# First projection pieces loaded among the gate pieces, a gate sent later, and a branch product on other accumulators

## The chip, the cores and the metric

The kernel runs on one core of a Trainium2 chip, as one program launched once. The metric is the device time in microseconds from the program's first to its last instruction with what the launch adds around them. A profiled execution gives a trace of every instruction and transfer. The engines are PE (TensorE), DVE (VectorE), ACT (ScalarE), POOL (GpSimd) and SP (SyncE, which here only issues loads).

## What is computed

A trunk of two layers over 256 tokens of width 1024, all in float32. Each layer has a token mixer and then a channel mixer, and each of the two is framed by a modulation that comes from a conditioning vector `c`:

```
shift, scale, gate = split(silu(c) @ w_mod + b_mod)
h   = normalize(x) * (1 + scale) + shift
x   = layer_norm(alpha * x + (1 + gate) * f(h))
```

The token mixer projects `h` by one matrix `w_in` (1920 columns), runs three branches on the result (stick-breaking attention, trailing pooling, sliding-window attention), projects each branch to 1024 columns, and merges them with gates:

```
qa, ka, va, u, qc, kc, vc = split(h @ w_in)
g_a, g_b, g_c = split(sigmoid(h @ w_gate))
merged = g_a * (y_a @ w_branch_a) + g_b * (y_b @ w_branch_b) + g_c * (y_c @ w_branch_c)
f(h) = merged @ w_out
```

The channel mixer is a dense SwiGLU in layer 0 and a top-2-of-8 expert SwiGLU in layer 1.

## The kernel before

All weights come from memory in pieces of 1 MB (128 partitions x 2048 floats) through a ring of `RING = 6` slots in `w_raw`. SP issues them in one fixed order. It waits, before each, until the slot's old piece is used: `piece_used` is counted up by DVE, `split_used` by PE, `shift_used` by PE for the shift pieces of the first modulation. As SP runs its queue in order, a load that waits holds back every load behind it.

A piece for an accurate product is split in two: ACT rounds it to `w_hi` (L577), DVE takes the rest to `w_lo` (L973, counts up `piece_used`), and PE makes three matmuls for each product: hi by hi, lo by hi and hi by lo (L1573 to L1575). The first `UNSPLIT = 3` pieces of a stretch are not split; PE multiplies them as they are (`project_raw`, L1584), each of these matmuls being two records in the trace. Tokens are in two tiles of 128 rows, t = 0 and 1.

The first modulation (`MOD0`) has twelve pieces. Its order is shift, scale, shift, scale, ... (eight pieces) and then the four gate pieces. The shift pieces are multiplied by PE (L1636), scale and gate pieces by DVE, four steps each into `mod_acc` (L1001, `mod_piece`). Then:

- PE sends shift and scale to all partitions (L1641, L1644); DVE's `modulate` makes `h` for tile 0 and tile 1 (L1054, L1057); PE transposes a tile (`h_transposed`, L1596); ACT keeps it as `actT_raw` (L606) and rounds it (L615).
- `send_gate` (L1609) sums the gate over the partitions into two banks of the accumulator memory, and ACT's `keep_gate` copies them to `gate1` (L599).
- After that GpSimd fills `mod_acc` anew for the next modulation: it waits for `gate1_ready`, issues four small loads, clears `mod_acc` (L478 to L480) and loads the next bias into it (L486, `acc_ready`). The pieces of that next modulation stand among the projection pieces, one after in3, one after the piece behind it, and so on. DVE's first step on the first of them waits for `acc_ready`, and DVE takes the pieces strictly in order.

The accumulator memory `ps` has eight banks of 512 columns. The projection of column block n and tile t goes to bank `2t + n % 2`. In the gate phase that leaves banks 0 and 2 (even blocks) and banks 1 and 3 (odd blocks) to be read by ACT's sigmoid (L746), which counts up `gate_ready` once for each tile: 12 in a layer, the last two for block 5, an odd one.

After the gates come the branch products. Their pieces carry the numbers j = 19 to 22. Piece 19 makes the products of branches 0 and 1 for the first 512 columns, piece 20 those for the other 512, pieces 21 and 22 those of branch 2. DVE multiplies the gates by the sums of each (`gated_branch`, L1190; `branch_read` counts the reads), merges them (L1255), and PE transposes the merged rows (L1756). A DVE helper `after(j)` is run three pieces behind the piece that DVE splits.

## Time and profile before

| what | value |
|---|---|
| median of three runs | 1730.75 us (1728.66 to 1731.32) |
| the profiled execution's own time | 1730.3 us |
| its span, first to last instruction | 1728.5 us |
| TensorE, busy | 1634.3 us, 95% of the span |
| VectorE, busy | 1360.6 us, 79% |
| ScalarE, busy | 1021.0 us, 59% |
| GpSimd, busy | 109.6 us, 6% |
| TensorE's mean granted clock | 0.985 |
| moved from memory | 510.46 MB, 301 GB/s over the span with what is written |

The times in the rows below are microseconds from the span's start. A timeline row is a run of like instructions: start, length, engine, line, operation, output and inputs, count, and in brackets the idle time ahead of it with what ended it. PEclk is the granted clock as a share of 2.4 GHz: 0.50 is 1.2 GHz, and a number between is a second in which both levels occurred. Instructions overlap a little in the records, since the end of a matmul is modelled.

### The profile page before, as it was taken

Reading aid. Unit: us, or ns where it says so; the run is one execution under the profiler, and the core shown is the slowest. Engines: PE = TensorE matmul, PEld = TensorE weight load, DVE = VectorE, ACT = ScalarE, POOL = GpSimd, SP = SyncE. Lnnn points to the kernel's source line nnn. Section 1 sums busy time; section 2 is a strip of 40 time slices with the busy share of each in tenths; the row PEclk is TensorE's granted clock in tenths of the full one; section 3 lists DMA queues with packets and bytes.
Section 4 is the critical chain, followed back from the end, with each engine's and each line's share of the span. In section 5 each row is a group of like instructions: output and inputs, shape, how many; then the busy total and the mean of one; then the engine's idle time right before and its main releaser. Section 6 shows DMA issues by size and latency. Waiting matters only on the chain.

```text
span 1728.5 us, 20762 instructions
## 1 busy us (share of the span) xinstructions
PE 1634.3 (95%) x7272; PEld 1274.2 (74%) x7273; DVE 1360.6 (79%) x1158; ACT 1021.0 (59%) x824; POOL 109.6 (6%) x76
## 2 busy tenths in 40 slices
PE   5999899999999999999999989999899999999895
PEld 2587767888587766777888768888687777788673
DVE  5696877665796877899888986565689999988798
ACT  1375434343375434778777775445577878877573
POOL 1200010000100002002001010000200200200200
PEclk9999999999999999999999999999999999999998
DMA  9775747775576644999999986666699999999993
GB/s 363 270 249 194 267 147 260 278 289 195 177 273 209 224 165 158 384 398 375 375 370 376 395 334 237 218 220 218 230 379 398 387 393 395 382 369 358 390 393 121
DMA packets 215859, 510.41 MB, mean 295 GB/s; under 512 B 12473, under 2 KB 16745, under 8 KB 215810
## 3 DMA queue, kind: packets, MB, share of 16 engines
q1 hardware_dynamic: 208770, 496.15, 79.0%
q0 software_dynamic: 7040, 13.60, 2.3%
q8 instruction: 31, 0.51, 0.1%
q14 instruction: 18, 0.14, 0.0%
HBM read 510.46 MB, written 10.49 MB: 301 GB/s over the span
## 4 chain that ended last, share of the span: by engine, by line
PE 76%; DVE 9%; DMA 7%; ACT 4%; issue 3%; SPq 0%; DVEq 0%; ACTq 0%
PE ps L1573 18%; PE ps L1575 17%; PE ps L1574 17%; PE ps L1579 5%; PE ps L1580 5%; DMA w_raw<-in_exp_w_dram 4%; PE ps L1584 4%; DVE w_lo L1426 3%; ACT w_hi L841 3%; PE ps L2110 2%; PE ps L2081 1%; DMA w_raw<-in_w_mod_mix_dram 1%; DVE w_lo L973 1%; PE ps L1615 1%; DMA w_raw<-in_w_gate_dram 1%
## 5 line engine op out<-in xcount | busy, mean ns | idle before, releaser
L1426 DVE TENSOR_TENSOR w_lo<-w_raw,w_hi 128x2048 fp32r<-128x2048 f32 x332 | 756.5, 2289 | 121.7 <-ACT w_hi L841 120.9
L841 ACT CAST w_hi<-w_raw 128x2048 fp32r<-128x2048 f32 x332 | 632.2, 1912 | 177.0 <-DMA w_raw<-in_exp_w_dram 161.8
L1573 PE MATMUL ps<-w_hi,actT_hi 128*128 128x512 f32 (+1 forms) x1464 | 581.0, 397 | 37.1 <-DVE w_lo L1426 15.9
L1575 PE MATMUL ps<-w_hi,actT_lo 128*128 128x512 f32 (+1 forms) x1464 | 567.6, 388 | 0.0
L1574 PE MATMUL ps<-w_lo,actT_hi 128*128 128x512 f32 (+1 forms) x1464 | 567.4, 388 | 0.0
L1573 PEld LDWEIGHTS ps<-w_hi,actT_hi 128*128 128x128 f32 x1464 | 277.2, 189 | 109.7 <-DVE w_lo L1426 30.1
L1575 PEld LDWEIGHTS ps<-w_hi,actT_lo 128*128 128x128 f32 x1464 | 277.1, 189 | 57.2
L1574 PEld LDWEIGHTS ps<-w_lo,actT_hi 128*128 128x128 f32 x1464 | 277.5, 190 | 53.8 <-issue 1.7
L973 DVE TENSOR_TENSOR w_lo<-w_raw,w_hi 128x2048 fp32r<-128x2048 f32 x82 | 187.5, 2288 | 91.2 <-ACT w_hi L577 91.0
L577 ACT CAST w_hi<-w_raw 128x2048 fp32r<-128x2048 f32 x82 | 156.0, 1907 | 110.3 <-DMA w_raw<-in_ffn_w_dram 59.4
L1579 PE MATMUL ps<-w_hi,gT_hi 128*128 128x512 f32 x448 | 178.4, 398 | 3.5 <-DVE gT_hi L1453 1.9
L1580 PE MATMUL ps<-w_lo,gT_hi 128*128 128x512 f32 x448 | 177.1, 395 | 0.0
L1001 DVE SCALAR_TENSOR_TENSOR mod_acc<-w_raw,c_act,mod_acc 128x512 f32<-128x512 f32 x176 | 120.0, 745 | 10.7 <-DMA w_raw<-in_w_mod_mix_dram 7.1
L1579 PEld LDWEIGHTS ps<-w_hi,gT_hi 128*128 128x128 f32 x448 | 84.1, 188 | 29.4 <-DVE w_lo L1426 5.6
L1580 PEld LDWEIGHTS ps<-w_lo,gT_hi 128*128 128x128 f32 x448 | 84.2, 188 | 19.1
L537 POOL DMA_INDIRECT by_row<-hbuf,row_of x14 | 32.1, 2293 | 817.6 <-DVE hbuf L1512 606.2
L1584 PE MATMUL ps<-w_raw,actT_raw 128*128 128x512 f32 x144 | 65.4, 609 | 4.8 <-DMA w_raw<-in_w_in_dram 4.0
L1584 PEld LDWEIGHTS ps<-w_raw,actT_raw 128*128 128x128 f32 x144 | 27.5, 194 | 38.9 <-issue 36.8
L1573 PE MATMUL ps<-w_hi,gT_hi 128*128 128x512 f32 x136 | 54.2, 398 | 1.2 <-DVE gT_hi L1453 1.2
L1574 PE MATMUL ps<-w_lo,gT_hi 128*128 128x512 f32 x136 | 54.1, 398 | 0.0
L1575 PE MATMUL ps<-w_hi,gT_lo 128*128 128x512 f32 x136 | 53.5, 394 | 0.0
L1579 PE MATMUL ps<-w_hi,actT_hi 128*128 128x512 f32 x112 | 44.4, 397 | 3.4 <-DVE actT_hi L1469 3.4
(288 smaller groups left out, 1230.7 us busy)
## 6 DMA issues: line engine op xcount, KB each, us to landing
w_raw<-in_exp_w_dram SPq DMA_DIRECT2D x336, 1024.0 KB, 7.6
w_raw<-in_ffn_w_dram SPq DMA_DIRECT2D x33, 1024.0 KB, 5.1
w_raw<-in_w_mod_mix_dram SPq DMA_DIRECT2D x24, 1024.0 KB, 7.5
w_raw<-in_w_mod_ffn_dram SPq DMA_DIRECT2D x24, 1024.0 KB, 6.6
w_raw<-in_w_gate_dram SPq DMA_DIRECT2D x24, 1024.0 KB, 5.1
w_raw<-in_w_in_dram SPq DMA_DIRECT2D x14, 1024.0 KB, 5.3
w_raw<-in_w_out_dram SPq DMA_DIRECT2D x8, 1024.0 KB, 5.1
w_raw<-in_w_branch_c_dram SPq DMA_DIRECT2D x4, 1024.0 KB, 7.4
```

The lines of the kernel that those rows point to most:

```text
L577: nc.scalar.copy(w_hi[:, (j - stretch.raw) % SPLIT, :], w_raw[:, slot, :]).then_inc(split_hi, 1)
L841: nc.scalar.copy(w_hi[:, i % SPLIT, :], w_raw[:, slot, :]).then_inc(split_hi, 1)
L973: TTn(w_lo[:, slot, :], w_raw[:, slot, :], w_hi[:, (j - stretch.raw) % SPLIT, :].bitcast(F32), ALU.subtract).then_inc(piece_used, 1)
L1001: ins = STT(acc, w[:, k, n * BANK:(n + 1) * BANK], c_act[:, 2 * (q % 4) + k:2 * (q % 4) + k + 1], acc, ALU.mult, ALU.add)
L1426: TTn(w_lo[:, slot, :], w_raw[:, slot, :], w_hi[:, i % SPLIT, :].bitcast(F32), ALU.subtract).then_inc(piece_used, 1)
L1573: MM(to, hi, w_h, start=first, stop=False)
L1574: MM(to, hi, w_l, start=False, stop=False)
L1575: return MM(to, lo, w_h, start=False, stop=last)
L1579: MM(to, packed, w_h, start=first, stop=False)
L1580: return MM(to, packed, w_l, start=False, stop=last)
L1584: return MM(to, actT_raw[:, k, t * P:(t + 1) * P], w_raw[:, slot, at * width:(at + 1) * width], start=first, stop=last)
L2110: MM(bank(n), gT_lo[:, 0, 2 * h + part, :], split_piece(EXPERT, i, part, n * BANK, D)[0], start=False, stop=False)
```

## The change

In the start, SP loads the three unsplit projection pieces in0, in1 and in2 among the gate pieces of the first modulation: in0 and in1 behind the first gate piece, in2 behind the second. DVE modulates tile 1 after the first gate piece instead of before it. PE transposes tile 1 and multiplies it by in0 before it sends the gate, which now goes to banks 6 and 7 instead of 2 and 3, and ACT keeps it after tile 1's rows. The attention scores of layer 0, which use those banks, wait for `gate1_ready`.

In both layers, the first branch's product goes to banks 0 and 2 and the second's to banks 1 and 3 (before: 0 and 1, 2 and 3). The first waits for ten of the twelve sigmoids, the second for all. The product of piece 20 that goes to banks 0 and 1 waits until two gated products have been read instead of one.

```diff
@@ -162,6 +162,7 @@
 
 MOD0 = Stretch(mod_stream())
 MOD0.n_used = MODS - MOD_SHIFT
+IN_AMONG_GATES = {2 * MOD_SHIFT: (0, 1), 2 * MOD_SHIFT + 1: (2,)}
 MIX = Stretch(mix_stream(), raw=UNSPLIT)
 DENSE_PANELS, _dense = ffn_stream(D_FF, True)
 DENSE = Stretch(_dense, raw=UNSPLIT, first_slot=MIX.n % RING)
@@ -195,6 +196,7 @@
 HALF_P = P // 2
 FOLDS = 2 * len(EXPERT_PANELS)
 LOGITS = 4
+BRANCH_BANKS = {"even": (0, 2), "odd": (1, 3), 0: (0, 1), 2: (2, 3), 4: (4, 5)}
 NOWHERE = 1 << 20
 TURN_FREE, TURN_LATE = (2, 3), (5, 7)
 
@@ -426,9 +428,11 @@
                 for d, s in pairs:
                     sp.dma_start(d, s).then_inc(raw_loaded[slot], 16)
 
-            def stream(stretch, base, layer, before, split_base, expert=None, mod_layer=None):
+            def stream(stretch, base, layer, before, split_base, expert=None, mod_layer=None, begun=0):
 
                 for i, piece in enumerate(stretch.pieces):
+                    if i < begun:
+                        continue
                     old = before.pieces[before.n - RING + i] if i < RING else stretch.pieces[i - RING]
                     if old[0] == "mod":
                         sp.wait_ge(piece_used, base + i + 1 - (0 if i < RING else stretch.raw))
@@ -454,9 +458,14 @@
                     else:
                         sp.wait_ge(shift_used, before // 2 + 1)
                 load(i % RING, piece, ("mix", 0))
-            sp.wait_ge(shift_used, MOD_SHIFT)
+                if i == 2 * MOD_SHIFT:
+                    sp.wait_ge(shift_used, MOD_SHIFT)
+                for m in IN_AMONG_GATES.get(i, ()):
+                    sp.wait_ge(piece_used, MOD0.n_used + m + 1)
+                    load(MIX.slot(m), MIX.pieces[m], 0)
             for layer in range(DEPTH):
-                stream(MIX, layer * LAYER_PIECES + MOD0.n_used, layer, DENSE if layer else MOD0, layer * LAYER_SPLITS, mod_layer=("ffn", layer))
+                stream(MIX, layer * LAYER_PIECES + MOD0.n_used, layer, DENSE if layer else MOD0, layer * LAYER_SPLITS, mod_layer=("ffn", layer),
+                       begun=0 if layer else UNSPLIT)
                 if layer < 1:
                     stream(DENSE, MOD0.n_used + MIX.n_used, 0, MIX, MIX.n_split, mod_layer=("mix", 1))
                 else:
@@ -654,8 +663,8 @@
             for t in range(TT):
                 root(t + 1, t)
             turned_h(0, 0, 0)
-            keep_gate(0, 0)
             turned_h(0, 1, 0)
+            keep_gate(0, 4)
 
             for layer in range(DEPTH):
                 sbase = layer * LAYER_SPLITS
@@ -1130,8 +1139,9 @@
                     mod_piece(MOD0, i, [0] * RING, 0, 0, 0)
                 if i == 2 * MOD_SHIFT - 1:
                     dve.wait_ge(mod_sent, 1)
-                    for t in range(TT):
-                        modulate(chain, t, 4)
+                    modulate(chain, 0, 4)
+                if i == 2 * MOD_SHIFT:
+                    modulate(chain, 1, 4)
             rest_of_turned(0, 0, raw_met, 1)
 
             for layer in range(DEPTH):
@@ -1183,11 +1193,11 @@
                     step(nc.vector.reciprocal(rden, den))
                     TTn(scores[:, :, :], scores[:, :, :], rden.unsqueeze(2).broadcast_to([P, 8, P]), ALU.mult).then_inc(prob_ready, 1)
 
-                def gated_branch(n, br, first_bank):
+                def gated_branch(n, br, banks):
 
                     for t in range(TT):
                         gate = gates[:, t, br * D + n * BANK:br * D + (n + 1) * BANK]
-                        ins = TTn(gate, gate, bank(first_bank + t), ALU.mult)
+                        ins = TTn(gate, gate, bank(BRANCH_BANKS[banks][t]), ALU.mult)
                     ins.then_inc(branch_read, 1)
                     dve.wait_ge(branch_read, layer * 6 + BRANCH_ORDER.index((br, n)) + 1)
 
@@ -1228,8 +1238,8 @@
                         dve.wait_ge(gate_ready, layer * 12 + 12)
                         yT_rest(1)
                         dve.wait_ge(split_used, sbase + 20 + SPLIT)
-                        gated_branch(0, 0, 0)
-                        gated_branch(0, 1, 2)
+                        gated_branch(0, 0, "even")
+                        gated_branch(0, 1, "odd")
                         for t in range(TT):
                             ins = TTn(gate_columns(0, 0, t), gate_columns(0, 0, t), gate_columns(0, 1, t), ALU.add)
                         step(ins)
@@ -1764,6 +1774,8 @@
                                 ins = TR(ps[:, 4 + c // 2, (c % 2) * SEQ + t * P:(c % 2) * SEQ + (t + 1) * P], proj[:, t, c * P:(c + 1) * P], ident)
                         ins.then_inc(aT_sent, 1)
                     if j == 5:
+                        if layer < 1:
+                            pe.wait_ge(gate1_ready, 1)
                         stick_scores()
                     if j == 9:
                         suffix_sums()
@@ -1810,11 +1822,14 @@
                         send_gate(2, 0)
                 ins.then_inc(raw_met, 1)
                 if layer < 1:
-                    pe.wait_ge(piece_used, MOD0.n_used + RING)
-                    send_gate(0, 0)
-                second_tile(layer * 2, 0)
+                    h_transposed(0, 1, 2)
+                else:
+                    second_tile(2, 0)
                 for i in range(UNSPLIT):
                     project_raw(i, 1).then_inc(split_used, 1)
+                    if layer < 1 and i == 0:
+                        pe.wait_ge(piece_used, MOD0.n_used + RING)
+                        send_gate(0, 4)
 
                 for i, piece in enumerate(MIX.pieces):
                     if piece[0] == "mod" or i < UNSPLIT:
@@ -1844,21 +1859,23 @@
                         if j == 19:
                             pe.wait_ge(yT_hi_ready, layer * 2 + 1)
                             pe.wait_ge(yT_lo_ready, layer * 2 + 1)
-                            pe.wait_ge(gate_ready, layer * 12 + 12)
+                            pe.wait_ge(gate_ready, layer * 12 + 10)
                         if j == 20:
                             pe.wait_ge(pT_ready, layer * 2 + 2)
                         if j == 21:
                             pe.wait_ge(yT_hi_ready, layer * 2 + 2)
                             pe.wait_ge(yT_lo_ready, layer * 2 + 2)
 
-                        groups = {19: [(0, (0, 1), 0, 0), (1, (2, 3), 2, 0)], 20: [(0, (0, 1), 4, 0), (1, (2, 3), 0, 1)],
+                        groups = {19: [(0, (0, 1), "even", 0), (1, (2, 3), "odd", 0)], 20: [(0, (0, 1), 4, 0), (1, (2, 3), 0, 2)],
                                   21: [(2, (4, 5, 6, 7), 2, 2)], 22: [(2, (4, 5, 6, 7), 0, 3)]}[j]
-                        for br, ks, first_bank, read in groups:
+                        for br, ks, banks, read in groups:
                             if read:
                                 pe.wait_ge(branch_read, layer * 6 + read)
+                            if banks == "odd":
+                                pe.wait_ge(gate_ready, layer * 12 + 12)
                             for t in range(TT):
                                 for k in ks:
-                                    ins = product(bank(first_bank + t), *chunk(k, t), *split_piece(MIX, i, k % 4, 0, BANK), k == ks[0], k == ks[-1])
+                                    ins = product(bank(BRANCH_BANKS[banks][t]), *chunk(k, t), *split_piece(MIX, i, k % 4, 0, BANK), k == ks[0], k == ks[-1])
                                     if j == 22 and t == 1 and k == 5:
                                         merged_T(0)
                         ins.then_inc(split_used, 1)
```

SP's queue from the first gate piece of the first modulation on, before (`w_mod_mix` is the first modulation, `w_in` the projection, `w_mod_ffn` the next modulation):

```order
L427 DMA w_raw<-in_w_mod_mix_dram 128x2x1024 [waits shift_used]
L427 DMA w_raw<-in_w_mod_mix_dram 128x2x1024 [waits piece_used]
L427 DMA w_raw<-in_w_mod_mix_dram 128x2x1024 [waits shift_used]
L427 DMA w_raw<-in_w_mod_mix_dram 128x2x1024 [waits piece_used]
L427 DMA w_raw<-in_w_in_dram 128x4x512 [waits piece_used,shift_used]
L427 DMA w_raw<-in_w_in_dram 128x4x512 [waits piece_used] x3
L427 DMA w_raw<-in_w_mod_ffn_dram 128x2x1024 [waits piece_used]
```

The same place of the changed kernel (its L429 is L427 before):

```order
L429 DMA w_raw<-in_w_mod_mix_dram 128x2x1024 [waits shift_used]
L429 DMA w_raw<-in_w_in_dram 128x4x512 [waits piece_used,shift_used]
L429 DMA w_raw<-in_w_in_dram 128x4x512 [waits piece_used]
L429 DMA w_raw<-in_w_mod_mix_dram 128x2x1024 [waits piece_used]
L429 DMA w_raw<-in_w_in_dram 128x4x512 [waits piece_used]
L429 DMA w_raw<-in_w_mod_mix_dram 128x2x1024 [waits shift_used]
L429 DMA w_raw<-in_w_mod_mix_dram 128x2x1024 [waits piece_used]
L429 DMA w_raw<-in_w_in_dram 128x4x512 [waits piece_used]
```

The first row in both is the first gate piece. Behind it two projection pieces come ahead of the second gate piece, and a third ahead of the last two.

PE from the raw product of in2 for tile 0 on, before (L1584 raw products, L1609 the gate's sums, L1596 transposes of tile 1):

```order
L1584 MATMUL ps<-w_raw,actT_raw 128x512 [waits raw_loaded2]
L1584 MATMUL ps<-w_raw,actT_raw 128x512 x3
L1609 MATMUL ps<-mod_acc,cst 128x512 [waits piece_used]
L1609 MATMUL ps<-mod_acc,cst 128x512
L1596 MATMUL ps<-cst,hbuf 128x128 [waits h_ready,gate1_ready]
L1596 MATMUL ps<-cst,hbuf 128x128 x3
L1596 MATMUL ps<-cst,hbuf 128x128 [waits h_ready]
L1596 MATMUL ps<-cst,hbuf 128x128 x3
L1584 MATMUL ps<-w_raw,actT_raw 128x512 [waits raw_loaded0,hT_raw_ready]
L1584 MATMUL ps<-w_raw,actT_raw 128x512 x3
```

The same place of the changed kernel (L1594, L1606 and L1619 are L1584, L1596 and L1609 before):

```order
L1594 MATMUL ps<-w_raw,actT_raw 128x512 [waits raw_loaded2]
L1594 MATMUL ps<-w_raw,actT_raw 128x512 x3
L1606 MATMUL ps<-cst,hbuf 128x128 [waits h_ready]
L1606 MATMUL ps<-cst,hbuf 128x128 x3
L1606 MATMUL ps<-cst,hbuf 128x128 [waits h_ready]
L1606 MATMUL ps<-cst,hbuf 128x128 x3
L1594 MATMUL ps<-w_raw,actT_raw 128x512 [waits raw_loaded0,hT_raw_ready]
L1594 MATMUL ps<-w_raw,actT_raw 128x512 x3
L1619 MATMUL ps<-mod_acc,cst 128x512 [waits piece_used]
L1619 MATMUL ps<-mod_acc,cst 128x512
```

The gate's two matmuls have moved behind the transposes of tile 1 and its product with in0, and the wait for `gate1_ready` ahead of the transposes is gone.

## Rows read from the trace of the kernel before

**Rows 1.** PE's timeline of the start: transposes, raw products, gate

```profile
43.22 12.23 PE L1584 MATMUL ps<-w_raw,actT_raw 128*128 128x512 f32 x24 [3.98 <-DMA w_raw<-in_w_in_dram]
55.29 1.88 PE L1609 MATMUL ps<-mod_acc,cst 128*128 128x512 f32 x4
58.34 1.09 PE L1596 MATMUL ps<-cst,hbuf 128*128 128x128 f32 x8 [1.18 <-ACT gate L599]
59.69 10.57 PE L1584 MATMUL ps<-w_raw,actT_raw 128*128 128x512 f32 x24 [0.25 <-ACT actT_raw L606]
...
75.58 1.03 PE L1764 MATMUL ps<-cst,proj 128*128 128x128 f32 x8
76.57 0.50 PE L1573 MATMUL ps<-w_hi,actT_hi 128*128 128x512 f32 x1
```

**Rows 2.** windows: busy by engine, then PEclk, DMA share, GB/s

```profile
44.00:45.00 1.00, 1.00 (x3) 0.34 (x2) 1.00 (x2) 0.00 (x0) 0.00 (x0) 0.61 0.77 100
...
47.00:48.00 1.00, 1.00 (x3) 0.28 (x2) 1.00 (x3) 0.00 (x0) 0.00 (x0) 0.68 1.01 363
...
556.00:557.00 1.00, 1.00 (x6) 0.67 (x4) 1.00 (x3) 1.00 (x1) 0.00 (x0) 0.61 0.62 229
...
563.00:564.00 1.00, 1.00 (x5) 0.81 (x5) 1.00 (x2) 0.66 (x1) 0.00 (x0) 0.97 0.00 0
676.00:677.00 1.00, 1.00 (x4) 0.71 (x4) 1.00 (x1) 0.23 (x1) 0.61 (x1) 0.50 0.02 4
30.00:40.00 10.00, 9.24 (x36) 5.66 (x34) 7.72 (x12) 1.13 (x3) 0.00 (x0) 1.00 1.03 405
```

**Rows 3.** SP's timeline: the first projection loads

```profile
31.34 1.93 SPq L427 DMA_DIRECT2D w_raw<-in_w_in_dram  x2
...
32.90 10.70 SPq L427 DMA_DIRECT2D w_raw<-in_w_in_dram  x2
```

**Rows 4.** PE's waits over the whole trace: total, times, longest

```profile
core 0 of [0], span 1728.5 us
...
PE ps L1573 <- ACT gates L746: 3.5, 2, 1.8
...
PE ps L1573 <- DVE w_lo L973: 0.4, 2, 0.2
```

**Rows 5.** DVE's timeline of the start

```profile
37.72 1.40 DVE L1054 SCALAR_TENSOR_TENSOR hbuf<-x_sb,mv,ps 128x512 f32<-128x512 f32 x2
...
40.47 10.68 DVE L1001 SCALAR_TENSOR_TENSOR mod_acc<-w_raw,c_act,mod_acc 128x512 f32<-128x512 f32 x16
...
71.57 2.73 DVE L1001 SCALAR_TENSOR_TENSOR mod_acc<-w_raw,c_act,mod_acc 128x512 f32<-128x512 f32 x4
74.22 2.29 DVE L973 TENSOR_TENSOR w_lo<-w_raw,w_hi 128x2048 fp32r<-128x2048 f32 x1
```

**Rows 6.** PE's timeline of the branch products in layer 0

```profile
186.42 0.47 PE L1573 MATMUL ps<-w_hi,actT_hi 128*128 128x512 f32 x1 [1.76 <-ACT gates L746]
...
195.44 0.50 PE L1573 MATMUL ps<-w_hi,actT_hi 128*128 128x512 f32 x1 [0.61 <-DVE gates L1190]
...
209.10 1.09 PE L1756 MATMUL ps<-cst,hbuf 128*128 128x128 f32 x8 [1.13 <-DVE hbuf L1255]
```

**Rows 7.** the load of in2, issued at 43.2

```profile
DMA to landing us min/median/max: 5.3/5.3/5.3
```

**Rows 8.** GpSimd's timeline: first small load, load of the next bias

```profile
58.58 0.54 POOL L499 DMA_DIRECT2D sinks_sb<-in_sinks_dram  x1 [6.59 <-ACT gate L599]
...
66.76 0.53 POOL L486 DMA_DIRECT2D mod_acc<-in_b_mod_ffn_dram  x1 [0.29 <-POOL mod_acc L480]
```

**Rows 9.** that bias, issue to landing

```profile
DMA to landing us min/median/max: 3.6/3.6/3.6
```

**Rows 10.** PE's timeline ahead of the experts

```profile
674.94 0.47 PE L1573 MATMUL ps<-w_hi,actT_hi 128*128 128x512 f32 x1 [3.24 <-issue]
```

**Rows 11.** DVE's timeline: the four gated products of layer 0

```profile
194.10 2.60 DVE L1190 TENSOR_TENSOR gates<-gates,ps 128x512 f32<-128x512 f32 x4
```

## The prediction

> **What bounds the kernel now.** I read the page first: TensorE is busy for 95% of the span, so what it waits for is what can be won. Next the list of PE's waits, then the first 80 us engine by engine, since one half of the change lives there, and then the stretch of the branch products, where the other half lives, once in each layer. Lines and times are those of the kernel before. I call the twelve modulation pieces q0 to q11 (q0 to q3 shift, q4 to q7 scale, q8 to q11 gate), the projection pieces in0, in1, ..., and the pieces of the next modulation, streamed among them, M0, M1, ... The order after in3 is M0, in4, M1, in5.
>
> In the start PE stands still for 3.98 us, from 39.24 to 43.22, until in0 has landed; the raw products of tile 0 take 12.23 us, then come the gate's matmuls at 55.29, a wait for ACT, the transposes of tile 1 at 58.34 and its raw products from 59.69, which take 10.57 us and end at 70.26 [rows 1]. The 12.23 us are longer than 10.57 for the same twelve products because the granted clock was 0.61 and 0.68 at the two edges and half between: some 3.4 us at 1.2 GHz, which cost 1.7 us [rows 2]. in0 was issued at 31.34, in1 at 32.90, but behind all of the gate's pieces [rows 3]. From there PE hardly waits for weights of this phase: its waits for w_lo of the streamed pieces sum to 0.4 us in the whole trace [rows 4]. But VectorE is right beside it: M0's four steps begin at 71.57, w_lo of in4 at 74.22 and takes 2.29 us, so it is ready at 76.51, and PE begins in4 at 76.57 [rows 1, 5].
>
> In the branch stretch PE waits twice for the sigmoid L746, 3.5 us in the two layers [rows 4], 1.76 of it in layer 0; then 0.61 for the first gated product and 1.13 for the merged rows [rows 6].
>
> **The change, part by part. 1, the loads.** q8 still goes out before. in0 is issued at 31.34 and in1 at 32.90, with the waits they had, but now only q8 is ahead of them. One piece alone lands 5.3 us after its issue [rows 7]; at 405 GB/s a further piece of 1.05 MB takes 2.6 us [rows 2]. So in0 lands at about 36.6, in1 at 39.2, q9, queued behind in1's wait, at 41.8. VectorE finishes tile 0's modulation where tile 1's began, 37.72 [rows 5], does q8 next (16 steps took 10.68, so 2.67 for four), and is done at 40.4. That releases in2, which lands at 45.7. q10 and q11, which stand behind in2's wait in SP's queue, follow at 48.3 and 50.9. VectorE modulates tile 1 until 43.2 (2.75 us, from 37.72 to 40.47), q9 until 45.9, then waits for q10: 48.3 to 51.0, q11 to 53.7. Before, q11 was done at 51.15 [rows 5]: the gate is 2.5 us later.
>
> **2, PE up to in3.** The first raw product can start at 39.5 (0.26 us after the transposes, as 58.34 plus 1.09 to 59.69) [rows 1]. At 3.44 us a piece it needs in2 at 46.4; in2 is there 0.7 earlier, so no wait, no idle 4 us before it, and I take the clock as full: 39.5 + 10.4 = 49.9. Tile 1 follows at once, 1.35 us for its transposes and ACT, then in0's product, 51.25 to 54.7. Its wait for q11 (53.7) is over by then, 1.0 us to spare. The gate's two matmuls take 1.75, and two raw pieces 6.9: PE is through at 63.4, against 70.26. That is 6.9 us earlier: the cover that the change seems to buy.
>
> **3, what is late next.** GpSimd reloads mod_acc with the next bias only after the gate has been kept, and VectorE's M0 waits for that and stands before w_lo of in4 on the same engine. From the gate's first matmul to GpSimd's next DMA it was 3.29 us (55.29 to 58.58), to the bias's issue another 8.18 (66.76), to its landing 3.6 [rows 1, 8, 9]. That chain of 15.1 us is kept whole, and the gate now starts at 54.7 instead of 55.29. The bias lands at 69.8; M0 goes from 69.8, w_lo of in4 is ready 4.94 us later (71.57 to 76.51), and PE starts in4 at 74.8: 1.8 us earlier than 76.57, not 6.9. PE has meanwhile done in3 and the transposes L1764 (70.26 to 76.57, 6.3 us) by 69.7 and idles 5.1 us. Then the clock: after 3.98 us of idle it fell [rows 2], and after 3.24 us at 674.94 too: half at 676 [rows 2, 10]; after 1.76 it did not show in the pitch of the products at 186.42 to 195.44 [rows 6]. So after 5.1 us it falls, and 3.4 us of half clock cost 1.7. in4 then ends where it would have, 0.1 us early. That work beside it is dense, so the 1.7 is on the path.
>
> The Trainium skill (TensorE: Matmul & The Clock Gate, Why this matters for your kernels) says the same against the change: keep PE free of long gaps between bursts, or the gate goes back to half. By it this stretch gains 0.1; by the chain alone, without the clock, it would gain 1.8.
>
> **4, the branch banks.** Branch 0's first product goes to banks 0 and 2, which the last but one gate piece leaves free, so it needs not wait for the last sigmoid: PE starts at 184.66 instead of 186.42. 36 matmuls then take 8.41 us (186.42 to 194.83, the start at 195.44 less its idle 0.61) [rows 6], so the half of the next piece that goes to banks 4 and 5 ends at 193.1. Its other half goes to banks 0 and 1, and bank 1 is now read by the second gated product: the wait is for branch_read 2 instead of 1. VectorE's four products are 194.10 to 196.70 [rows 11], and nothing that they wait for has moved (they stand behind ACT's and VectorE's own work, not behind PE). PE starts at 196.75 instead of 195.44, 1.3 us later, and has idled 3.6 us. Of the 1.3 the wait of 1.13 before L1756 takes most: 0.2 is left. Without a fall of the clock each layer loses 0.2, 0.4 for both.
>
> 3.6 us of idle lies between the 3.24 and the 3.98 after which the clock fell. A fall costs 1.7, with the slack at L1756 already spent. But whether a fall comes and how long it is has varied: after the same 64-row products it lasted 3.4 us in layer 0 and 6.8 in layer 1 (0.61 at 556, 0.97 at 563) [rows 2], and a program moved by 1 or 2 us may win such a piece or lose it. So I count net falls, not places.
>
> **Sum.** Start -0.1, banks +0.4, one net fall +1.7: +2.0 us. Against the profiled run's own 1730.3 (span 1728.5 and 1.8 around it) [rows 4] that is 1732.3; its distance to the median 1730.75 is 0.45, inside the three runs' spread, and I set the sum on the median: 1732.7.
>
> **The rivals.** *No net fall*: -0.1 + 0.4 = +0.3, 1731.0. For it: PE idles only 3.6 us, and layer 1 may get back the longer fall. *Two net falls*: +3.7, 1734.4. For it: both idles are longer than 3.24; against it: it takes both layers and no return. *Long falls, slower than before*: in the branch stretch the clock stays low for 6.8 us as at 556, not 3.4: 3.4 us a layer, -0.1 + 0.4 + 6.8 = +7.1, 1737.8. One layer is enough to pass the limit of slower. For it the row at 556; against it both falls after an idle PE that I can place lasted 3.4 or less well over that.
>
> *The start pays*: the bias lands sooner or the clock holds after 5.1 us. The shortest chain that rows allow is a landing at once, -3.6; then PE idles 1.5 us, no fall, and the start gains 5.4; a landing after half the time gives 3.6 with a fall or without. Between: start -1.8 to -3.6, banks +0.4, 1728.4 as its middle. The Trainium skill (DMA: Bandwidth & Descriptors, Anatomy of one DMA) gives about 2.0 us fixed plus bytes at 436 GB/s for GpSimd's path; for 12 KB that makes 2.0 instead of 3.6, an estimate from that page, and the start would gain 1.7 instead of 0.1. The trace disagrees for this very transfer.
>
> *The chain does not bind*: if M0 were not before in4's w_lo in time, the whole 6.9 would be kept: 1730.75 - 6.9 + 0.4 = 1724.3. Against it the order of VectorE in the code. *Loads collide*: in2 or q10, q11 land late since SP stands in in2's wait. A us of delay of q11 beyond 54.7 delays the gate, the bias and in4 by one; 3.5 us of it would make it slower. It has 1.0 of slack, so I count it with the slow tail.
>
> **How the numbers follow.** About 0.2%, 3.5 us, is what a measurement of this kernel can tell from no change. One net fall 0.30 (1732.7), none 0.24 (1731.0), two 0.20 (1734.4), the start pays 0.12 (1728.4), the chain does not bind 0.06 (1724.3), long falls or late loads 0.08 (1737.8). Faster by over 3.5: the chain case and half of the paying start, 0.12. Slower: the last case and just under half of "two", which lies at the limit of 1734.2, 0.17. Same: 0.71. The range from 1728.2 to 1735.2 leaves out the chain case, the long falls and some of the edges, 2 in 10; the likeliest case's own is 1731.5 to 1734.
>
> **What would show it.** PE's first raw product near 39.5 and no low clock at 44 to 48; in2 landed before 46.4; the gate's matmuls near 54.7; in4 near 74.8 with an idle of some 5 us in front, ended by w_lo, and half clock behind it; VectorE's M0 held by the bias's DMA. In the branch stretch no wait for L746, and one of 3.6 us in place of 0.61 until L1190 has read; L1756 no longer waiting. I am wrong if M0 starts well before 69, if PE keeps its clock behind either idle, or if q11 ends after 55.

## The result, and the profile after

The changed kernel takes 1737.16 us (median of 22 runs, 1731.17 to 1742.07) where the kernel before takes 1731.62 (22 runs, 1728.48 to 1739.22): a ratio of 1.0030, with a 95% interval of 1.0022 to 1.0039. That is 5.5 us or 0.3% slower, past the 0.2% that I called the limit, and 2 us above the top of my range, which stood on the median of three runs, 0.9 us below that of the 22. The profiled execution took 1737.82 us, with a span of 1736.0. One run of `p2_before_padded`, a kernel further down, took 2054.64 us at a mean granted clock of 0.748; it is left out of its figures.

The clock is lower over all runs, not only in the profiled one. A run's mean granted clock is 0.978 to 0.984 in the 22 runs of the changed kernel, 0.9807 in the mean, and 0.980 to 0.986 in the 122 runs of the kernel before that were timed beside the experiments, 0.9839 in the mean. The difference of 0.0032 is some 5.5 us of the span, an estimate from these means, and as large as the loss; a part of it falls on idle time and costs nothing.

PE's timeline of the start, to be read beside [rows 1] (the bracket is the idle time before a row and what ended it):

```profile
core 0 of [0], span 1736.0 us
...
39.29 10.68 PE L1594 MATMUL ps<-w_raw,actT_raw 128*128 128x512 f32 x24 [0.25 <-ACT actT_raw L615]
49.81 1.04 PE L1606 MATMUL ps<-cst,hbuf 128*128 128x128 f32 x8
51.09 3.70 PE L1594 MATMUL ps<-w_raw,actT_raw 128*128 128x512 f32 x8 [0.25 <-ACT actT_raw L615]
54.63 1.88 PE L1619 MATMUL ps<-mod_acc,cst 128*128 128x512 f32 x4
56.35 7.03 PE L1594 MATMUL ps<-w_raw,actT_raw 128*128 128x512 f32 x16
...
68.70 1.03 PE L1774 MATMUL ps<-cst,proj 128*128 128x128 f32 x8
...
76.22 0.80 PE L1583 MATMUL ps<-w_hi,actT_hi 128*128 128x512 f32 x1 [6.48 <-DVE w_lo L982]
```

The wait for in0 is gone, the raw products run without a gap, and PE is 6.8 us ahead when they end (63.4 against 70.26). Then it stands for 6.48 us, and in4 starts at 76.22, only 0.35 us before its old 76.57. Who holds it is seen on GpSimd, in the landing of its bias, and on VectorE, which correspond to [rows 8], [rows 9] and [rows 5]:

```profile
57.92 0.54 POOL L508 DMA_DIRECT2D sinks_sb<-in_sinks_dram  x1 [2.89 <-ACT gate L608]
...
66.13 0.53 POOL L495 DMA_DIRECT2D mod_acc<-in_b_mod_ffn_dram  x1 [0.29 <-POOL mod_acc L489]
```
```profile
DMA to landing us min/median/max: 5.1/5.1/5.1
```
```profile
71.22 2.74 DVE L1010 SCALAR_TENSOR_TENSOR mod_acc<-w_raw,c_act,mod_acc 128x512 f32<-128x512 f32 x4 [6.44 <-DMA mod_acc<-in_b_mod_ffn_dram]
73.88 2.28 DVE L982 TENSOR_TENSOR w_lo<-w_raw,w_hi 128x2048 fp32r<-128x2048 f32 x1
```

The bias is issued 0.6 us earlier than before and lands 5.1 us later instead of 3.6, so M0 begins at 71.22, nearly where it did. What the idle does to the clock is in the windows (columns as in [rows 2]: the last three figures are the granted clock, the DMA share and GB/s; a clock between 0.50 and 1.00 means that both levels occurred in the stretch). Of the changed kernel, and then of the kernel before:

```profile
44.00:45.00 1.00, 1.00 (x4) 0.41 (x3) 1.00 (x3) 0.00 (x0) 0.00 (x0) 1.00 1.09 422
47.00:48.00 1.00, 1.00 (x3) 0.38 (x2) 0.00 (x0) 0.00 (x0) 0.00 (x0) 1.00 1.00 410
72.00:76.00 4.00, 0.00 (x0) 0.00 (x0) 4.00 (x4) 1.52 (x4) 0.00 (x0) 0.50 0.70 189
76.00:82.00 6.00, 5.79 (x14) 4.58 (x15) 6.00 (x8) 2.40 (x3) 0.00 (x0) 0.50 0.39 160
202.00:206.00 4.00, 4.00 (x13) 3.10 (x12) 2.95 (x3) 0.00 (x0) 0.00 (x0) 0.63 0.00 0
597.00:604.00 7.00, 5.77 (x14) 4.53 (x15) 5.01 (x6) 1.71 (x1) 0.00 (x0) 0.54 0.00 1
```
```profile
core 0 of [0], span 1728.5 us
...
76.00:82.00 6.00, 6.00 (x30) 4.84 (x29) 6.00 (x8) 1.74 (x3) 0.00 (x0) 1.00 0.86 295
202.00:206.00 4.00, 4.00 (x20) 3.30 (x19) 3.93 (x5) 1.92 (x1) 0.00 (x0) 1.00 1.03 384
592.00:600.00 8.00, 8.00 (x36) 6.58 (x36) 7.86 (x11) 2.18 (x2) 0.00 (x0) 1.00 0.59 211
```

The low clock at 44 to 48 is gone, and a new one covers the idle and the first 5.8 us of in4: 14 matmuls from 76 to 82 where the kernel before has 30. Both branch stretches have one too, in layer 0 (202 to 206) and a longer one in layer 1 (597 to 604), where before had 1.00. PE's waits over the whole trace show the wait that moved, beside [rows 4]; the wait for the sigmoid is gone from the list:

```profile
PE ps L1583 <- DVE gates L1200: 7.4, 2, 3.7
PE ps L1583 <- DVE w_lo L982: 6.7, 2, 6.5
```

And in layer 1 VectorE now waits for PE at its next gated product, which it did not before:

```profile
603.75 2.60 DVE L1200 TENSOR_TENSOR gates<-gates,ps 128x512 f32<-128x512 f32 x4 [1.93 <-PE ps L1585]
```

To see where time is lost I took the start of the same instruction in both traces. "Rotation" is VectorE's first step after the start's projections, "yc(1)" ACT's copy in front of the branch products, "merged" its copy of the merged rows' transposes behind them:

| place | before | after | behind |
|---|---|---|---|
| rotation, layer 0 | 98.26 | 100.67 | 2.41 |
| yc(1), layer 0 | 184.70 | 188.52 | 3.82 |
| merged, layer 0 | 210.22 | 215.66 | 5.44 |
| yc(1), layer 1 | 580.76 | 586.18 | 5.42 |
| merged, layer 1 | 606.27 | 614.51 | 8.24 |
| span | 1728.5 | 1736.0 | 7.5 |

So in these two executions 2.4 us come from the start, 1.4 from the stretch up to the branches (the products of 64 rows at 164, where the low clock lasts longer: PEclk of 163 to 171 is 0.57, before 0.79), 1.6 and 2.8 from the two branch stretches.

### The profile page after: what moved, and what is told of

It reads as the page before. It is cut to its first block, busy times and chain, and to the rows that moved or that the text cites. A ratio compares the mean times of both kernels' runs of the same rounds, so it can differ in the third digit from the quotient of the medians.

```text
span 1736.0 us, 20762 instructions
## 1 busy us (share of the span) xinstructions
PE 1640.9 (95%) x7272; PEld 1280.7 (74%) x7273; DVE 1360.9 (78%) x1158; ACT 1020.6 (59%) x824; POOL 104.9 (6%) x76
## 4 chain that ended last, share of the span: by engine, by line
PE 75%; DVE 9%; DMA 8%; ACT 4%; issue 3%; POOL 0%; SPq 0%; DVEq 0%; ACTq 0%
PE ps L1583 18%; PE ps L1585 17%; PE ps L1584 17%; DMA w_raw<-in_exp_w_dram 6%; PE ps L1589 5%; PE ps L1590 5%; PE ps L1594 3%; DVE w_lo L1436 3%; ACT w_hi L850 3%; PE ps L2127 2%; PE ps L2098 1%; DMA w_raw<-in_w_mod_mix_dram 1%; DMA w_raw<-in_w_gate_dram 1%; DVE stats L1032 1%; PE ps L1729 1%
## 5 line engine op out<-in xcount | busy, mean ns | idle before, releaser
L1584 PE MATMUL ps<-w_lo,actT_hi 128*128 128x512 f32 (+1 forms) x1464 | 571.0, 390 | 0.0
L1584 PEld LDWEIGHTS ps<-w_lo,actT_hi 128*128 128x128 f32 x1464 | 279.9, 191 | 54.8 <-issue 1.7
L1594 PE MATMUL ps<-w_raw,actT_raw 128*128 128x512 f32 x144 | 64.0, 597 | 1.1 <-ACT actT_raw L615 1.0
L1584 PE MATMUL ps<-w_lo,gT_hi 128*128 128x512 f32 x136 | 54.1, 398 | 0.0
L1594 PEld LDWEIGHTS ps<-w_raw,actT_raw 128*128 128x128 f32 x144 | 26.8, 190 | 34.3 <-issue 31.1
```

The source lines that it names most:

```text
L1584: MM(to, hi, w_l, start=False, stop=False)
L1594: return MM(to, actT_raw[:, k, t * P:(t + 1) * P], w_raw[:, slot, at * width:(at + 1) * width], start=first, stop=last)
```

## The experiments

All were timed in five rounds beside the kernel before (f1 has 5 runs, m1 6, the others 11 or 12). I give the median and then the ratio to that kernel with its 95% interval; the ratio goes by all runs and need not be the quotient of the medians. A difference of two ratios below is given in us of 1731.6, its interval worked out from the two. "Theory" and "rival" are as each expectation names them. My theory after the result: both waits act as forecast, and each costs mainly through the clock.

**The parts alone.** `s1_start_only` is the change without its banks, `b1_banks_only` the banks without the loads. The edit of s1, against the changed kernel ("..." stands for lines left out; the second product's own wait for the twelve sigmoids, which the first now has, falls away):

```diff
-BRANCH_BANKS = {"even": (0, 2), "odd": (1, 3), 0: (0, 1), 2: (2, 3), 4: (4, 5)}
+BRANCH_BANKS = {"even": (0, 1), "odd": (2, 3), 0: (0, 1), 2: (2, 3), 4: (4, 5)}
...
-                            pe.wait_ge(gate_ready, layer * 12 + 10)
+                            pe.wait_ge(gate_ready, layer * 12 + 12)
...
-                  20: [(0, (0, 1), 4, 0), (1, (2, 3), 0, 2)],
+                  20: [(0, (0, 1), 4, 0), (1, (2, 3), 0, 1)],
```

> The changed kernel with the branch banks as before; loads, tile 1 and the gate as changed. Theory (chain and clock): the bias of the next modulation holds VectorE until 71, PE idles 6.5 us before in4, the clock falls for 10 us behind it, and the stretch ends 2.4 us later than before; total +2.4 us against the kernel before (+1.5 to +3.5). Rival (the loads and the gate pay, all of the loss is from the banks): -2 to -6 us. Rival (the start costs more, through what comes later): +5 us or more.

> The kernel before with the branch banks alone changed. Theory (the wait has moved to the second gated product and the clock falls behind it): no wait for the sigmoid, 3.5 us or more of idle before the second half of piece 20, half clock for 3.4 to 6.8 us behind it, merged rows 1.7 to 3 us later in each layer; total +3 to +5 us. Rival (the banks are neutral and the start costs all): within 1 us of before. Rival (the banks gain what the sigmoid cost): -1 to -3 us.

s1: 1733.14 us, 1.0019 (1.0007 to 1.0031). b1: 1731.42, 1.0005 (0.9997 to 1.0014). Together 1.0024 where the whole is 1.0030, within the intervals. So the start alone costs 3.3 us (1.2 to 5.4), within what I expected, and the banks alone 0.9 us (0.5 less to 2.4 more than before) where I had expected 3 to 5. s1 has the chain of the whole change: in4 at 76.26 behind 6.50 us of idle, a bias that lands in 5.1. But its low clock ended 3 us sooner: 19 matmuls from 72 to 82 us instead of 14. b1 has the idle of 3.7 in both layers, and each of its branch stretches, from yc(1) to merged, takes 27.1 us instead of 25.5. But the same trace is only 0.1 us behind at the first expert pieces, since a low clock that the kernel before has at 645 to 652 is missing there, and b1's mean granted clock over its runs is 0.984, as that of the kernel before. So b1 has falls in the branch stretches and gets them back elsewhere.

**The same waits with the clock held.** Small matmuls, whose results nothing reads, fill the idle in front of in4 (`s2_start_kept_busy`, on s1) and in front of the branch product (`b2_banks_kept_busy`, on b1); `f1_changed_kept_busy` is the changed kernel with both:

```diff
+                                if j == 20:
+                                    pe.wait_ge(yc_ready, layer * 2 + 2)
+                                    stay_busy(4, 6)
                                 pe.wait_ge(branch_read, layer * 6 + read)
...
+                    if layer < 1 and j == 3:
+                        pe.wait_ge(gate1_ready, 1)
+                        stay_busy(12, 6, C_IDENT, C_PAST)
```

> As s1, but PE makes twelve matmuls of the identity into a free bank, 5.4 us, after the transposes of piece 3, where it would wait for in4. Their result is not used. Theory: the idle shrinks to about 1 us, in4 starts as late as in s1 (76.2), but at full clock; its end comes 2.9 us sooner than in s1, so the stretch is 0.3 to 0.5 us ahead of the kernel before, total -0.5 us. Rival (the clock is not what costs; the lateness of in4 is): the same as s1, +2.4 us.

> As b1, but PE makes four matmuls of the identity into bank 6, 3.4 us, before it waits for the second gated product in piece 20. Theory: no fall of the clock in the branch stretch; the merged rows come 0 to 0.3 us later than before in each layer, total +0.3 us. Rival (the later start of the second half is what costs, not the clock): +1.3 us a layer, +2.6 us.

> The changed kernel whole, with both fillers (twelve matmuls before in4, four in piece 20 of each layer; their results are not used). Nothing of the waits is taken away, only the clock is held. Theory (the loss is the clock's): -1 to -3 us against the kernel before, so 5 to 8 us under the changed kernel. Rival (the moved waits themselves cost): +2 to +5 us, as the changed kernel.

s2: 1729.95, 0.9988 (0.9975 to 1.0002). b2: 1730.52, 0.9991 (0.9980 to 1.0001); its branch stretches take 25.53 and 25.53 us, those of before 25.52 and 25.51. So in the trace the moved wait costs nothing in itself, not even the 0.2 us a layer of my sum; the 1.6 us a layer of b1 are the clock. Over the runs b2 is 2.4 us below b1 (0 to 5). In s2 in4 starts at 76.39, as late as in s1, and the kernel is 5.4 us below s1 (2 to 9): what the start costs comes through the clock. f1: 1724.54 (five runs, 1722.31 to 1727.13), 0.9966 (0.9953 to 0.9979), 11 us below the changed kernel by the ratios. That is more than the change lost, so something else was in it. It comes back below.

**The chain.** `s3_m0_one_later` (on s1) has M0 behind in4, which should free in4's w_lo of the bias; `s4_bias_first` (on s1) lets GpSimd reload mod_acc before its small loads; `m1_before_m0_later` is s3's edit on the kernel before:

```diff
-MOD_BEFORE = (4, 5, 6, 7, 8, 12, 13, 14, 17, 18, 21, 22)
+MOD_BEFORE = (5, 6, 7, 8, 8, 12, 13, 14, 17, 18, 21, 22)
```

```diff
                 gp.wait_ge(gate1_ready, layer * 2 + 1)
+                gp.wait_ge(gate_sent, layer * 2 + 1)
+                gp.sem_inc(acc_free, 1)
+                fresh_acc(I["b_mod_ffn"][bass.ds(layer, 1), :], layer * 2 + 1)
...
-                gp.wait_ge(gate_sent, layer * 2 + 1)
-                gp.sem_inc(acc_free, 1)
-                fresh_acc(I["b_mod_ffn"][bass.ds(layer, 1), :], layer * 2 + 1)
```

> As s1 (banks as before), with the first piece of the next modulation behind in4 instead of ahead of it (the others one place later too, the fifth where it was; both layers). Theory (the bias chain holds in4 only because M0 stands before it on VectorE): PE starts in4 right behind the transposes at 69.8, no idle of 6.5 us, no fall there, in5 waits under 1.5 us for its w_lo; -4 to -6 us against the kernel before. Rival (something else behind it, a load or a cast, holds PE as long): within 1 us of s1, +2 us.

> As s1, with GpSimd's four small loads issued behind the reload of mod_acc and not ahead of it (both layers). Theory: the bias is issued 2.5 us sooner, at 63.6, and lands at 67 to 68.7; in4 starts at 72 to 73.8, PE idles 2.3 to 4 us instead of 6.5, the fall is shorter or absent; -2 to -4 us against s1, so -2 to 0 against the kernel before. Rival (the landing, not the issue, is what is late, held by loads of 1 MB): in4 starts within 0.5 us of s1.

> The kernel before with the pieces of the next modulation one place later, as in s3, and nothing else. Theory: there M0 was done just in time, so the move alone changes nothing in the start: within 1 us of before. Rival (the new place pays by itself, whatever the loads do): -2 us or more, and s3's gain is not the change's.

s3: 1729.58, 0.9986 (0.9973 to 1.0000), a gain of 2.4 us where 4 to 6 were expected. PE no longer waits for in4's w_lo, and its rotation begins at 94.55, 3.7 us before that of the kernel before. VectorE's rows, of s3:

```profile
65.14 2.29 DVE L982 TENSOR_TENSOR w_lo<-w_raw,w_hi 128x2048 fp32r<-128x2048 f32 x1
71.84 2.74 DVE L1010 SCALAR_TENSOR_TENSOR mod_acc<-w_raw,c_act,mod_acc 128x512 f32<-128x512 f32 x4 [4.42 <-DMA mod_acc<-in_b_mod_ffn_dram]
```

w_lo of in4 is done before the bias, and M0 still waits for it. That shows the chain: the order on VectorE ties in4 to the bias. s4: 1731.72, 1.0004 (0.9990 to 1.0018), 2.6 us below s1 (its interval reaches from 6 us less to 0.6 more); the bias goes out at 63.97, lands in 5.2, and in4 starts at 74.16, 2.1 us before s1's, as the chain says. Of m1 I had expected little: it took 1738.67, 1.0053 (1.0035 to 1.0071), and neither theory forecast that. Its rotation is 1.1 us late and it waits 2.31 us for a w_lo at 107.58; by the branch stretch of layer 1 it is 8.0 us behind. So the place of M0 has a price of its own. That s3 paid it out of what it gained is likely and not shown.

**Further trials.** `n1_before_kept_busy` is the kernel before with eight small matmuls where PE waits for in0; `b3_second_half_other_banks` is b1 with the second half of the piece in banks 6 and 7, which asks no gated product (VectorE reads it there, and PE waits at the piece's start for `yc_ready` and `yb_ready`; those lines are left out below); `f2_busy_bias_first` is f1 with s4's edit and 7 small matmuls instead of 12; `f3_start_busy_bias_first` is that without the banks and their matmuls:

```diff
             h_transposed(0, 0, 0)
+            stay_busy(8, 2, C_IDENT, C_PAST)
```

```diff
-                        groups = {..., 20: [(0, (0, 1), 4, 0), (1, (2, 3), 0, 2)],
+                        groups = {..., 20: [(0, (0, 1), 4, 0), (1, (2, 3), 6, 0)],
```

> The kernel before, with eight matmuls of the identity into bank 2, 3.6 us, while PE waits for in0 (their result is not used). Theory (the clock after an idle PE costs what the rows of before show): no low clock at 44 to 48, the first raw products end 1.7 us sooner, and VectorE's chain behind them keeps it: -1.7 us against before, -1 to -2. Rival (what comes behind takes it back): within 0.5 us of before.

> As b1, but the second half of piece 20 goes to banks 6 and 7, which are free there, so it waits for no gated product; VectorE reads it there. No filler. Theory (the idle of 3.7 us that the moved wait makes is what lets the clock fall): piece 20 runs through, PE waits about 1 us before piece 21 and up to 2.7 before the merged rows, which come as early as before; no fall between, 0 us against before, -1 to +1.5. Rival (the fall comes wherever PE has a few us less to do in this stretch): merged rows 1.7 to 3 us late in each layer, as b1.

> The changed kernel whole, with GpSimd's small loads behind the reload of mod_acc, seven identity matmuls before in4 (3.1 us) and four in piece 20 of each layer. Theory (the chain sets in4's start, the fillers hold the clock): in4 at 74 instead of 76.2, no fall behind it; -7 to -9 us against before, 1.5 to 2.5 better than the changed kernel kept busy. Rival (what is won at in4 is taken back by the 1 MB loads behind it): -6 us, as that one.

> As the last, but with the branch banks as before and without the four fillers there. Theory (the branch banks win nothing by themselves, since VectorE's gated products set the merged rows): within 1 us of the last. Rival (the earlier start of piece 19 is worth its 1.8 us a layer once the clock is held): 3 us above the last.

n1: 1730.00, 0.9985 (0.9972 to 0.9998); the low clock at 44 is gone, and the gain of 2.6 us holds the 1.7 that was expected in its interval. b3: 1733.22, 1.0010 (0.9994 to 1.0027): in layer 0 the idle of 3.7 us is split in two, 1.08 before the piece that follows and 2.48 before the merged rows, whose stretch takes 26.4 us; that of layer 1 takes 25.5 as before. Over the runs it can't be told from b1 or from the kernel before. f2: 1728.99, 0.9971 (0.9954 to 0.9988), spread from 1720.91 to 1734.68. f3: 1731.26, 0.9995 (0.9983 to 1.0008), 4 us above f2 (0.5 to 8) where I had expected 1 at most. f2 should have beaten f1 and did not. The ranking of these kernels does not follow their waits.

**What f1 had besides.** I laid the starts of w_lo of all 332 expert pieces side by side. Up to the experts f1 and the kernel before are within 1 us (merged of layer 1: 606.54 and 606.27). At 1235 f1 is 0.4 us ahead, at 1253, 6.3 us, and it stays there. At that place PE waits for "issue", for nothing that the profile can name. Of the kernel before, and of its version p2 below:

```profile
core 0 of [0], span 1728.5 us
...
1237.77 0.77 PE L1573 MATMUL ps<-w_hi,actT_hi 128*128 128x512 f32 x1 [4.99 <-issue]
```
```profile
core 0 of [0], span 1724.0 us
...
1233.76 0.47 PE L1573 MATMUL ps<-w_hi,actT_hi 128*128 128x512 f32 x1 [0.83 <-issue]
...
1237.75 0.50 PE L1573 MATMUL ps<-w_hi,actT_hi 128*128 128x512 f32 x1 [0.34 <-issue]
```

The DMA view of the kernel before, 1233 to 1238, has a load of the instruction queue in it, 16 KB, of which there are 31 in the whole trace:

```profile
q8 instruction: 1, 0.02, 1.2%
```

Behind this wait the clock is low too. From 1236 to 1243, before and in p2:

```profile
1236.00:1243.00 7.00, 5.24 (x14) 4.17 (x15) 2.54 (x2) 2.42 (x2) 4.01 (x2) 0.55 0.51 171
```
```profile
1236.00:1243.00 7.00, 6.66 (x30) 5.19 (x29) 4.65 (x3) 5.87 (x5) 4.50 (x2) 1.00 1.00 363
```

So the wait looks like one for the engine's own code, and would move with the number of instructions in front. Three kernels tell this from the clock. They have 20 small matmuls in front of PE's waits for the first modulation pieces, where it idles anyway; 20 is the number of matmuls that f1 has added before this place. `p1_changed_padded` is the changed kernel, `p2_before_padded` the kernel before, `p3_kept_busy_padded` is f1, each with them:

```diff
                 slot = 2 * shift % RING
+                stay_busy(5, 0, C_IDENT, 128)
                 pe.wait_ge(raw_loaded[slot], MOD0.loads[2 * shift])
```

> The changed kernel with 20 small matmuls (128 columns, results unused) in front of PE's waits for the first modulation pieces, five before each of four, where PE stands idle for 1.4 to 10 us anyway. They are as many as the kernel f1_changed_kept_busy has added in front of the experts, but they hold the clock behind none of the waits that the change makes. Theory A, the clock alone: all of f1's gain over the changed kernel came from the clock, so this one stays at the changed kernel's 1737, with an idle of 4.6 us at 1244 before the first expert product of layer 1 as there. Theory B, where the instructions lie: some 5 us of f1's gain came from the wait 'issue' at that place (4.6 us in the changed kernel, 0.45 in f1, with loads of the instruction queue beside it), which comes and goes with the number of instructions in front: this one comes to 1731 to 1733, with that wait under 1 us.

> The kernel before with the same 20 small matmuls in the same idle time. Theory A, the clock alone: no change, ratio 0.999 to 1.001. Theory B, where the instructions lie: the wait of 4.99 us at 1237.77 shrinks to under 1 us or moves to another place, and the time is either 3 to 6 us shorter or the same, according to whether it is paid elsewhere.

> f1_changed_kept_busy (the changed kernel with twelve small matmuls in front of in4 and four in front of the branch product of each layer) with the 20 of p1 as well: the clock is held as in f1, the instructions lie 20 matmuls further on. Theory A, the clock alone: 1724.5 as f1. Theory B, where the instructions lie: the wait for 'issue' near 1237 comes back in one place or another, 3 to 6 us, and the time is 1728 to 1731, which would then be what the clock alone gives back, 6 to 9 us of the changed kernel's 1737.

p1: 1728.62 (1725.05 to 1737.43), 0.9994 (0.9978 to 1.0009). p2: 1725.94, 0.9974 (0.9961 to 0.9988). p3: 1733.34, 1.0009 (0.9996 to 1.0022). What theory B says of the wait holds in all three: the waits for issue fell from 4.99 to 0.83 and 0.34 us in p2 and from 4.64 to 0.38 and 0.58 in p1, and p3, 20 matmuls further on than f1, has 4.85 again. The times that it gave for p1 (1731 to 1733) and p3 (1728 to 1731) were both missed by some 2 us, p1 below and p3 above. p2 makes the kernel before 4.5 us faster with matmuls that do nothing, and its trace has all of that at this one place: 0.5 us behind the kernel before at 1234, 4.5 ahead at 1258. The ratios to the kernel before, by what the trace shows at this place:

| | wait of 4.6 to 5.0 us for issue | without it |
|---|---|---|
| before | 1 | 0.9974 (p2) |
| changed | 1.0030 | 0.9994 (p1) |
| changed, clock held | 1.0009 (p3) | 0.9966 (f1) |

Down the columns: holding the clock behind the change's two waits gives back 3.6 us (1 to 6) and 4.8 us (1 to 8). From left to right the code's place gives 4.5 us (2 to 7), 6.2 (3 to 9) and 7.4 (4 to 11), which the intervals don't tell apart. In the traces it is the wait and the low clock behind it: from before it to behind it p2 gains 5.0 us on the kernel before, and p1 6.2 on the changed kernel, where 3.7 are the wait's. The kernel before, the changed kernel and p3 have half clock there, p1, p2 and f1 have none.

How much a low clock costs differs as well. With 6.22 us of idle before in4, p1's low clock ended before 79, and its second branch stretch had an idle of 3.7 us and no fall at all (PEclk of 594 to 604, of p1):

```profile
594.00:604.00 10.00, 10.00 (x46) 8.26 (x45) 9.86 (x12) 1.91 (x1) 0.00 (x0) 1.00 0.74 272
```

That execution was the fastest of p1's twelve; seven of them took 1725 to 1729 us and five 1731 to 1738. s2 and f2 do not stand in this table: their waits for issue moved and did not vanish (9.2 and 9.6 us in sum, before 8.2; s2 has 4.93 at 794, f2 4.91 at 1354). What I had read from f1 alone, 11 us for the clock, was more than twice too much.

## Why the prediction was wrong

**The loads.** Right. The first raw product was forecast at 39.5 and came at 39.29, no low clock at 44 to 48, the gate's matmuls at 54.7 and 54.63, the end of the raw pieces at 63.4 and 63.4.

**What is late next.** The mechanism was right and is shown by s3 and s4: the gain of 6.8 us ends at the bias that M0 waits for. Its size was off by one term, "to its landing 3.6": it was 5.1. The bias now goes out at 66.13, among loads that the faster PE has released (DMA share 1.02 from 66 to 72 us). That the loads beside it are the cause is borne out by all 17 kernels: with the old order of loads it lands in 3.6 to 4.1 us, and the engines move 234 to 267 GB/s in the first 2 us behind its issue; with the new order it lands in 4.8 to 5.2, at 367 to 406 GB/s. The chain from the gate's matmuls to M0 is 16.6 us, not 15.1. So in4 starts at 76.22, 1.4 us after my 74.8, and PE idles 6.5 us instead of 5.1. The Trainium skill (DMA: Bandwidth & Descriptors, Anatomy of one DMA) gives about 2.0 us fixed for such a transfer. The trace agrees where nothing else is loading: the same instruction of layer 1, issued at 455.84 at a DMA share of 0.02, lands in 2.0 us, in the kernel before and in the changed one. In the start the traces show 3.6 and 5.1, so the rival that the prediction built on 2.0 was further off than my own term.

**The clock at the start.** "So after 5.1 us it falls, and 3.4 us of half clock cost 1.7": it fell, but the low clock covers the idle and 5.8 us of in4, which costs 2.9. The term of the start, -0.1, was a gain of 1.8 less 1.7; measured it is a gain of 0.35 less 2.9, so +2.5, and the table above has 2.4 at the rotation. Half of the error is the bias, half the clock. This is the step that failed for certain: s1, the start alone, costs 3.3 us (1.2 to 5.4) where my sum had -0.1, and s2, which holds the clock there, is no slower than the kernel before (0.9975 to 1.0002).

**The banks.** The wait of 1.76 us became one of 3.70 (forecast 3.6), and no wait for L746 and none before L1756 is left (1.13), all as forecast. That it costs 0.2 a layer without a fall is shown to be right enough by b2 (0.0). The second step that failed is "So I count net falls, not places" with its term +1.7: I took one net fall of 1.7 us for both layers and for all that the shift in time might bring. The changed kernel's profile has a fall in each layer, the second nearly 7 us long, and they cost 1.6 and 2.8 us, 4.4 where my sum had 0.4 + 1.7 = 2.1; the longer fall at the 64-row products costs 1.4 more. This is read from one execution. b1 has a fall in each layer too, yet gives them back, and costs 0.9 us (at most 2.4) over its runs, so for the banks alone one net fall was no bad count. It failed for the kernel as a whole, whose mean clock is 0.0032 below that of before.

**Sum.** Worked out again with the sizes of the profiled execution: start +2.4, banks +4.4, the 64-row products +1.4, in all +8.2, as the table shows at the last branch; the span ends 7.5 later and the medians differ by 5.5. My sum was +2.0. The case that came is between my "two net falls" (+3.7) and "long falls" (+7.1), and I gave the two together 0.28. I set the fall's price by the shortest row that I had, though the row at 556 to 563 showed one twice as long. Of the 5.5 us, some 4 are given back when the clock is held behind both waits (3.6 and 4.8, each to within some 3 us). With the wait for code gone the change costs 3.5 us (p1 against p2, from nothing to 7).

**Left open.** Why the same idle brings a fall of a different length, or none; why b1 gets its falls back and the whole change does not; and what makes the place of M0 cost as much as m1 shows.

## What to carry to other kernels

A wait that is moved in front of TensorE has two prices: its time, which often has cover, and the half clock behind it, which comes out of the work that follows and has none; take the longest fall that the trace of before shows as one end of that price, and expect one behind each such idle, though a program that is moved may get one back elsewhere. Before an edit's gain is believed, look in the changed trace for waits with no releaser far from the edit: here 20 idle matmuls moved the time by 4.5 and 6.2 us, as much as the change did. And a load that is moved frees the loads behind it, so the small transfer on which the next step hangs can land later than the row of before says.

## What the runs showed of the hardware

**A wait for code.** PE stands 4.99 us before the first product of an expert at 1237.77, with a 16 KB load of the instruction queue inside the idle. 20 more matmuls in front make it 0.83 and 0.34. In other kernels such a wait showed elsewhere, 4.93 us at 794 (s2) and 4.91 at 1354 (f2). The granted clock is low behind it: 0.55 from 1236 to 1243, where p2 has 1.00. The Trainium skill (Runtime: NRT & Kernel Launch, Instruction fetch mechanics) says that code comes in pages of 16 KB and that a branch to a page that isn't loaded stalls until it has been fetched. The size agrees (31 loads, 0.51 MB), and the experts' code branches on row counts; that this very wait is a taken branch no run here shows.

**The length of a low clock.** Behind 6.2 to 6.5 us of idle before in4 the granted clock came back after some 6 us of work in the changed kernel (14 matmuls at half clock in 76 to 82) and within 3 in s1 and p1. Behind 3.7 us of idle in layer 1 it was low for nearly all of 597 to 604 in the changed kernel and not at all in p1. The runs of one kernel differ in the same way: the fastest of the changed kernel, 1731.17 us, had a mean granted clock of 0.984, the slowest, 1742.07, one of 0.978.

**The landing of a small transfer.** The bias, 12 KB from GpSimd's queue, lands 2.0 us after its issue when nothing else is loading (455.84, DMA share 0.02), in 3.6 at 255 GB/s beside it (66.76, kernel before) and in 5.1 at 395 GB/s (66.13, changed kernel). The windows of the 2 us behind its issue, of the kernel before and then of the changed one, and the landing of the one at 455.84:

```profile
66.76:68.76 2.00, 2.00 (x6) 0.85 (x5) 0.00 (x0) 1.90 (x3) 0.53 (x1) 1.00 0.93 255
455.84:457.84 2.00, 2.00 (x6) 0.85 (x5) 0.20 (x1) 1.77 (x1) 0.52 (x1) 1.00 0.02 6
```
```profile
66.13:68.13 2.00, 2.00 (x11) 1.65 (x10) 0.00 (x0) 0.10 (x1) 0.53 (x1) 1.00 1.07 395
```
```profile
DMA to landing us min/median/max: 2.0/2.0/2.0
```
